# A hybrid decoder trunk on one core: block compression contracted over 128 rows, with shifted copies of keys and values

## The reference, cut to what matters

```python
CMP_LEN, CMP_STRIDE, dh, G = 32, 16, 64, 2
def _compress(x, idx, pe, w1, w2):          # x: (B, T, G, dh)
    blocks = x[:, idx] + pe[:, None, :]      # 31 windows of 32 positions, 16 apart
    blocks = jnp.swapaxes(blocks, 2, 3).reshape(B, idx.shape[0], G, -1)
    return jax.nn.silu(blocks @ w1) @ w2     # w1: (32*64, 64), w2: (64, 64)
kc = _rms_norm(_compress(k_cmp, cmp_idx, cmp_pe[0], cmp_w1[0], cmp_w2[0]), k_g[0])
vc = _compress(v_cmp, cmp_idx, cmp_pe[1], cmp_w1[1], cmp_w2[1])
```

## Time and profile before

| | |
|---|---|
| runs | 2716.51, 2718.03, 2720.47 us; median 2718.03 |
| span of the profiled execution | 2716.9 us (its own time is not among the three; the median lies 1.1 us above the span) |
| TensorE busy, matmul records | 2664.1 us, 98% of the span |
| granted clock of TensorE, mean | 0.995 |
| VectorE, GpSimd, ScalarE busy | 1326.2, 1230.2, 1100.5 us |
| the compression's matmuls (line 763) | 256 records in each of the 2 layers |

### The profile page before, as it was taken

How to read it: one execution, slowest core, us unless ns; L and a number is a source line. 1 busy time by engine, 2 the same in 40 slices (tenths; PEclk the granted TensorE clock), 3 DMA queues, 4 the chain that set the end, 5 groups by cost and what they waited for, 6 DMA issues and landing times.

```text
span 2716.9 us, 36975 instructions
## 1 busy us (share of the span) xinstructions
PE 2664.1 (98%) x13132; PEld 2137.3 (79%) x13132; DVE 1326.2 (49%) x1834; ACT 1100.5 (41%) x1664; POOL 1230.2 (45%) x616
## 2 busy tenths in 40 slices
PE   8999999989999999999999999999899999999999
PEld 6888888766678868888888888887667788788887
DVE  5221258786535554252541212777865364543533
ACT  5322242446644454222342223434476445542222
POOL 4444456672235424444444434567522354344443
PEclk9999999999999999999999999999999999999999
DMA  4334433222224313333333353432122342233332
GB/s 133 95 99 113 115 98 87 70 55 55 55 78 117 109 47 107 94 99 95 91 95 101 93 132 92 111 79 68 49 55 63 86 124 85 62 101 101 93 100 78
DMA packets 493612, 243.41 MB, mean 90 GB/s; under 512 B 49468, under 2 KB 491174, under 8 KB 493478
## 3 DMA queue, kind: packets, MB, share of 16 engines
q1 hardware_dynamic: 492960, 241.49, 32.0%
q10 hardware_dynamic: 518, 0.13, 0.0%
HBM read 239.46 MB, written 2.10 MB: 89 GB/s over the span
## 4 chain that ended last, share of the span: by engine, by line
PE 65%; issue 16%; POOL 8%; DVE 5%; ACT 3%; POOLq 2%; DVEq 1%; ACTq 0%; DMA 0%; SPq 0%
PE pg L636 20%; PE pg L639 19%; PE pg L642 19%; POOL wL L585 7%; PE pA L706 2%; DVE convb L1740 1%; PE pA L911 1%; PE pA L858 1%; POOLq L612 1%; POOLq L614 1%; DVE prob L1902 0%; POOL wsn L610 0%; ACT prob L1156 0%; ACT wH L1156 0%; ACT hH L1156 0%
## 5 line engine op out<-in xcount | busy, mean ns | idle before, releaser
L585 POOL TENSOR_TENSOR wL<-raw,wH 128x1024 fp32r<-128x1024 f32 (+1 forms) x472 | 1084.9, 2300 | 1453.2 <-ACT wH L1156 1449.4
L636 PE MATMUL pg<-gxH,wH 128*128 128x512 f32 (+1 forms) x2448 | 960.6, 392 | 3.6 <-DVE gxL L1601 3.1
L642 PE MATMUL pg<-gxH,wL 128*128 128x512 f32 (+1 forms) x2448 | 948.7, 388 | 0.0
L639 PE MATMUL pg<-gxL,wH 128*128 128x512 f32 (+1 forms) x2448 | 944.1, 386 | 0.0
L1156 ACT ACTIVATE wH<-raw 128x1024 fp32r<-128x1024 f32 (+1 forms) x472 | 475.8, 1009 | 834.3 <-PE pg L642 673.5
L636 PEld LDWEIGHTS pg<-gxH,wH 128*128 128x128 f32 x2448 | 461.0, 188 | 110.7 <-issue 18.4
L639 PEld LDWEIGHTS pg<-gxL,wH 128*128 128x128 f32 x2448 | 461.2, 188 | 93.6 <-issue 7.1
L642 PEld LDWEIGHTS pg<-gxH,wL 128*128 128x128 f32 x2448 | 461.0, 188 | 93.2 <-issue 3.9
L642 PE MATMUL pg<-hH,wL 128*128 128x512 f32 x992 | 392.7, 396 | 0.0
L636 PE MATMUL pg<-hH,wH 128*128 128x512 f32 x992 | 390.5, 394 | 1.5 <-DVE hL L1657 1.5
L639 PE MATMUL pg<-hL,wH 128*128 128x512 f32 x992 | 390.6, 394 | 0.0
(11 more groups left out here) (234 smaller groups left out, 2208.8 us busy)
## 6 DMA issues: line engine op xcount, KB each, us to landing
raw<-in_ffn_wi SPq DMA_DIRECT2D x352, 256.0 KB, 3.1
raw<-in_w_in SPq DMA_DIRECT2D x200, 256.0 KB, 3.3
raw<-in_ffn_wo SPq DMA_DIRECT2D x128, 256.0 KB, 3.0
raw<-in_ffn_wo SPq DMA_DIRECT2D x64, 192.0 KB, 2.6
raw<-in_xkv SPq DMA_DIRECT2D x32, 256.0 KB, 3.0
raw<-in_w_out SPq DMA_DIRECT2D x32, 256.0 KB, 3.0
raw<-in_sgu_out SPq DMA_DIRECT2D x32, 128.0 KB, 2.2
raw<-in_conv_out SPq DMA_DIRECT2D x32, 128.0 KB, 2.2
```

Of the source, the lines that this page charges most:

```text
L585: pool.tensor_tensor(wL[:, s % 4, 0:n, :], raw[:, s % 2, 0:n, :], wH[:, s % 4, 0:n, :].bitcast(F32), ALU.subtract)\
L636: mm(o, wH[:, s, k, :], rh(k), start=(k == 0), stop=False)
L639: mm(o, wH[:, s, k, :], rl(k), start=False, stop=False)
L642: last = mm(o, wL[:, s, k, :], rh(k), start=False, stop=(k == kt - 1))
```

## The change

The 32 positions of a window are contracted in pairs. Even positions' channels take rows 0 to 63, odd positions' channels rows 64 to 127, and both groups stand side by side as 62 columns. For that, each of the two halves needs each group's data: group 0 at even positions lies where it is needed, group 1 at odd positions too, and the other two are copied by four SBUF-to-SBUF transfers for each layer (`kvx`), the odd one shifted by a position. Keys' sums go to rows 0 to 63 of bank 2, values' to rows 64 to 127 of bank 3. `w1` is loaded once, with even positions on one half of the partitions and odd ones on the other; `w2` shrinks in the same way, and the small loads go from 18 to 12. The windows are built by eight additions of 64 x 496 instead of two of 128 x 992: four where the two stood, four after the keys' `normed(l, 2, ...)`, behind a wait for the copies. SyncE waits for `kv_in` between the loads of unit `U_KV + 4` and those of `U_KV + 5`, and issues the four copies there.

```diff
-        w1 = [[big[:, 0:2 * T], big[:, 2 * T:4 * T]], [prob[:, 0:2 * T], prob[:, 4 * T:6 * T]]]
-        w1 = [[half.rearrange("p (j e) -> p j e", j=HL) for half in both] for both in w1]
+        w1 = [t.rearrange("p (j e) -> p j e", j=HL) for t in (big[:, 0:2 * T], prob[:, 0:2 * T])]
+        kvx = [big[:, (2 + i) * T:(3 + i) * T] for i in range(2)]
         blk = [big[:, (4 + 2 * i) * T:(4 + 2 * i) * T + CMP_LEN * NCMP]
-               .rearrange("p (j n) -> p j n", j=CMP_LEN) for i in range(2)]
+               .rearrange("p (j g n) -> p j g n", j=HL, g=KVG) for i in range(2)]
...
-                        rows = cmp_w1[l][i].rearrange("(j d) e -> d j e", d=DH)
-                        for x in range(2):
-                            load_small(w1[i][x][r, :, :], rows[:, x * HL:(x + 1) * HL, :])
-                        load_small(w2[r, i, :], cmp_w2[l][i])
+                        rows = cmp_w1[l][i].rearrange("(j b d) e -> b d j e", b=2, d=DH)
+                        load_small(w1[i][r, :, :], rows[half])
+                    load_small(w2[r, 0, :], cmp_w2[l][half])
...
                 for i in range(6):
                     unit(l, U_KV + i, 0, cols_of(win, C_KV + i * P))
+                    if i == 4:
+                        sp.wait_ge(kv_in, risen(kv_in, l, 1))
+                        for j in range(2):
+                            sp.dma_start(kvx[j][0:DH, :], kvc[DH:P, j, :]).then_inc(kvx_in, 16)
+                            sp.dma_start(kvx[j][DH:P, 0:T - 1], kvc[0:DH, j, 1:T])\
+                                .then_inc(kvx_in, 16)
...
-                for i in range(2):
-                    for j in range(CMP_LEN):
-                        for g in range(KVG):
-                            r = slice(g * DH, (g + 1) * DH)
-                            last = mm(pA[r, 2 + g, 32 * i:32 * i + NCMP],
-                                      w1[i][j // HL][r, j % HL, :], blk[i][r, j, :],
-                                      start=(j == 0), stop=(j == CMP_LEN - 1))
+                for j in range(HL):
+                    for i in range(2):
+                        last = mm(pA[i * DH:(i + 1) * DH, 2 + i, 0:KVG * NCMP], w1[i][:, j, :],
+                                  blk[i][:, j, :, :].rearrange("p g n -> p (g n)"),
+                                  start=(j == 0), stop=(j == HL - 1))
                 last.then_inc(cmp1, 1)
...
-                    mm(pA[r, 3, 0:NCMP], w2[r, 0, :], hc[r, 0, 0:NCMP], start=True, stop=True)
+                    mm(pA[r, 3, 0:NCMP], w2[0:DH, 0, :], hc[0:DH, g, 0:NCMP], start=True, stop=True)
                 for g in range(KVG):
-                    r = slice(g * DH, (g + 1) * DH)
-
-                    last = mm(pA[0:NCMP, 3 - g, P:P + DH], hc[r, 1, 0:NCMP],
-                              w2[r, 1, :], start=True, stop=True)
+                    last = mm(pA[0:NCMP, 2, P + g * DH:P + (g + 1) * DH], hc[DH:P, g, 0:NCMP],
+                              w2[DH:P, 0, :], start=True, stop=True)
...
                 scaled(kvc[:, 1, :], l, U_KV + 1)
                 dve.drain()
 
+                dve.drain().then_inc(kv_in, 1)
+
+                def windows(i, g, half, src):
+
+                    src = bass.AP(tensor=src.tensor, offset=src.offset,
+                                  ap=[src.ap[0], [2, HL], [CMP_STRIDE, NCMP]])
+                    r = slice(half * DH, (half + 1) * DH)
+                    pe_ = par[r, P_PE + i * HL:P_PE + (i + 1) * HL]
+                    pe_ = bass.AP(tensor=pe_.tensor, offset=pe_.offset,
+                                  ap=[pe_.ap[0], [1, HL], [0, NCMP]])
+                    return TTt(blk[i][r, :, g, :], src, pe_, ALU.add)
+
                 for i in range(2):
-                    src = kvc[:, i, :]
-                    src = bass.AP(tensor=src.tensor, offset=src.offset,
-                                  ap=[src.ap[0], [1, CMP_LEN], [CMP_STRIDE, NCMP]])
-                    pe_ = par[:, P_PE + i * CMP_LEN:P_PE + (i + 1) * CMP_LEN]
-                    pe_ = bass.AP(tensor=pe_.tensor, offset=pe_.offset,
-                                  ap=[pe_.ap[0], [1, CMP_LEN], [0, NCMP]])
-                    last = TTt(blk[i], src, pe_, ALU.add)
-                last.then_inc(blk_in, 1)
+                    windows(i, 0, 0, kvc[0:DH, i, :])
+                    windows(i, 1, 1, kvc[DH:P, i, 1:T])
                 conv(2)
...
                 normed(l, 2, kT[:, 0, :], col(P_NK + 1))
+                dve.wait_ge(kvx_in, risen(kvx_in, l, 16 * 4))
+                for i in range(2):
+                    windows(i, 1, 0, kvx[i][0:DH, :])
+                    last = windows(i, 0, 1, kvx[i][DH:P, :])
+                last.then_inc(blk_in, 1)
                 scaled(kT[:, 1, :], l, U_KV + 4)
                 squares(kT[:, 1, :])
                 v_copied(0)
```

More of the change, by code:

```diff
@@ L116, in trunk @@
         eps = sb("eps", [P, 1])
-        w2 = sb("w2", [P, 2, DH])
+        w2 = sb("w2", [P, 1, DH])
         hc = sb("hc", [P, 2, 32])
@@ L129, in trunk @@
         mst = sb("mst", [P, 2])
-        NP_ROWS = 126
+        NP_ROWS = 94
         NPAR = NP_ROWS + 4 * CONV_W
@@ L281, in trunk @@
         hid_l = sig("hid_l", 2 * FT)
-        small = sig("small", 16 * 18)
+        small = sig("small", 16 * 12)
         memld = sig("memld", 16 * 1)
+        kv_in = sig("kv_in", 1)
+        kvx_in = sig("kvx_in", 16 * 4)
         blk_in = sig("blk_in", 1)
@@ L733, in v_rows @@
                     last.then_inc(v_tr, 1)
-                pe.wait_ge(small, risen(small, l, 16 * 18))
+                pe.wait_ge(small, risen(small, l, 16 * 12))
                 turn(pA[:, 0, 0:4 * CONV_W], cwt[0:4 * CONV_W, :], 4 * CONV_W).then_inc(cw_tr, 1)
@@ L1259, in _ @@
                               (nsa_k_norm.rearrange("l a c -> a l c"), P_NK),
-                              (cmp_pe.rearrange("l i a c -> i a l c")[0], P_PE),
-                              (cmp_pe.rearrange("l i a c -> i a l c")[1], P_PE + CMP_LEN)):
+                              (cmp_pe.rearrange("l i (a b) c -> i b a l c", b=2)[0, half], P_PE),
+                              (cmp_pe.rearrange("l i (a b) c -> i b a l c", b=2)[1, half], P_PE + HL)):
                     n = g.shape[0]
@@ L1297, in _ @@
                     last = act.activation(hc[r, :, 0:NCMP],
-                                          pA[r, 2 + g, 0:64].rearrange("p (i n) -> p i n", i=2)
-                                          [:, :, 0:NCMP], ACT.Silu)
+                                          pA[r, 2 + g, 0:KVG * NCMP]
+                                          .rearrange("p (g n) -> p g n", g=KVG), ACT.Silu)
                 last.then_inc(cmp_act, 1)
@@ L1810, in _ @@
                 dve.tensor_copy(kcn[:, 0:NCMP], pA[:, 3, 0:NCMP])
-                for g in range(KVG):
-                    dve.tensor_copy(vcs[0:NCMP, g, 0:DH], pA[0:NCMP, 3 - g, P:P + DH])
+                dve.tensor_copy(vcs[0:NCMP, :, 0:DH],
+                                pA[0:NCMP, 2, P:2 * P].rearrange("p (g d) -> p g d", g=KVG))
                 squares(kcn[:, 0:NCMP], NCMP)
```

## The result

The changed kernel takes 2724.8 us (median of 12 runs, 2722.56 to 2729.53); the kernel before takes 2718.03 beside it. The ratio is 1.0021, with a 95% interval from 1.0014 to 1.0028. It is slower by a little over what a measurement of this kernel can tell from no change, where 2711.8 and a gain were forecast. The profiled execution took 2722.56 us, 1.8 more than its span. It is the fastest of the twelve, 2.2 us under their median, so its rows show a little less than what the change costs in a typical execution.

The account below looks back on a forecast made before the run. TensorE, its matmul records covering 98% of the span, was taken to bound the kernel. A layer: -5.6 + 0.1 + 2.4 = -3.1 us; both layers -6.2, so 2718.0 becomes 2711.8 us, range 2706.5 to 2717.5.

Parts of the forecast that it names:

- back-to-back ones of VectorE keep their turn: VectorE and GpSimd: two-SBUF-input instructions exclude each other, and consecutive VectorE ones are not interrupted; read from a 3.93 us wait.
- the layout by hand: VectorE before the third statistic: late additions 456.1 to 459.9, squares end 462.9, statistic at 463.0 instead of 460.15.
- Rival 4: Late additions: GpSimd gets turns between them, pauses about 5.5 us, statistic 8 us late, 2723.0 us; chance 0.07.
- The loss at the statistic: TensorE waiting for VectorE's late squares at the third statistic: 2.4 us a layer taken, 0.7 to 4 in the forecast.
- rival 3: Third statistic: both waits on GpSimd are full, a loss of about 5 us a layer, 2717.0 us; chance 0.10.
- The compression: TensorE's compression matmuls: 32 pairs at 59 ns, 2.0 us instead of 7.58, saving 5.6 us a layer.
- rivals 2 and 5: Compression: 2, pairs take 4.1 us instead of 2.0, 2716.0 us, 0.10; 5, loads don't overlap, saving 0.5, 2722.0, 0.03.
- `w2`: Four small TensorE matmuls with w2: values' two now share rows and columns, +0.1 us a layer.
- The copies: Four SBUF-to-SBUF copies for each layer: landed by 445 us or so, waiting for them costs nothing.
- Unit `U_KV + 5`: Its load, held behind the copies: ready about 449 to 451 us, TensorE takes it at 454.6, so hidden.
- Smaller loads: Small loads, 12 instead of 18: SyncE's issue 6.1 us shorter, 1 MB a layer saved, no gain taken.

Follow-up runs that it names:

- The cut additions of the kernel before: Kernel before the change, its two additions of 128x992 cut into four of 128x496 in the same place; 2718.94 us, one run.
- filled stop: Changed kernel plus six 128x512 matmuls on constants on TensorE ahead of the third statistic; 2723.12 us, ratio 1.0014.
- merged: Changed kernel with keys' and values' additions merged, two early and two late of 64 x 992 at the same places; 2720.45 us, ratio 1.0006.
- without taps: Changed kernel with GpSimd's convolution taps starting seven units later, leaving only subtractions beside the late additions; 2728.56 us, ratio 1.0034.
- halves: Changed kernel with each group of four additions reordered, those on the same partition half together; 2724.16 us, ratio 1.0019.

## Why the prediction was wrong

**The step that failed is the rule "back-to-back ones of VectorE keep their turn".** It was read from one pair, where a tap waited 3.93 us, and the layout by hand ran the late four from 456.1 to 459.9 on it. They started at 456.25, close to the forecast, and ran until 464.45, since GpSimd had a turn at each. The cut additions of the kernel before show that the rule fails even where it was read, from the third addition on.

Rival 4 had this mechanism, and its total of 2723.0 us came near the measured 2724.8. That is in part luck. It put all of its 8 us into the wait for the squares; the wait was 5.8, the pauses in the additions some 4.1 instead of 5.5, and the 2.0 or 1.6 us of clock that filled up the sum were not in it. It was given 0.07, since none of the rows showed more than two in a row against a GpSimd with work queued. But the trace from which the rows were taken had such a case, in the attention of the first layer: four subtractions of 128 x 512 back to back, each with two SBUF inputs (VectorE first, then GpSimd).

```profile
564.54 0.69 DVE L1946 TENSOR_TENSOR hL<-big,hH 128x512 fp32r<-128x512 f32 x1
565.14 1.80 DVE L1946 TENSOR_TENSOR hL<-big,hH 128x512 fp32r<-128x512 f32 x1
566.86 0.68 DVE L1946 TENSOR_TENSOR hL<-big,hH 128x512 fp32r<-128x512 f32 x1
567.47 1.09 DVE L1946 TENSOR_TENSOR hL<-big,hH 128x512 fp32r<-128x512 f32 x1
...
564.59 1.81 POOL L613 TENSOR_TENSOR convb<-convb,wsn 128x512 f32<-128x512 f32 x1
566.56 1.46 POOL L610 TENSOR_SCALAR wsn<-convb,par 128x512 f32<-128x512 f32 x1 [0.17 <-issue]
```

A tap's sum gets in ahead of the second, which takes 1.80 us; a tap's product waits through the third and gets in ahead of the fourth, which takes 1.09. So before any run the rule already stood against a counterexample in its own trace, and rival 4's chance should have been far higher.

The Trainium skill, in "SBUF — State Buffer" (section "SBUF: two separate sides"), says only that a lock is held for one whole instruction. Nothing in it says that the next in the same queue keeps it; that was added by the prediction, from the 3.93 us, which span one addition and the next. The trace agrees with the page, in the 1.26 to 3.02 us of the late four, and not with the addition.

**A term was missing.** The loss at the statistic was sized 2.4 us, with 0.7 to 4 in the forecast and about 5 in rival 3. A stop also costs clock: 2.0 us in the first layer and 1.6 in the second. The forecast had TensorE at the same speed behind a stop as in front of it. With the longer stop, 7.4 to 7.8 us came where 2.4 stood.

**The sum, term by term for a layer.** The compression -5.6 as forecast (2.01 us measured for 32 pairs, 63 ns a pair over all). The reading of the earlier trace rows held, that such records do not pay for their load and their stream one after the other, which by the prediction's working would have been 7.1 us: rivals 2 and 5 fell. `w2` +0.1 as forecast. Statistic +7.8 and +7.4 instead of +2.4. Together +2.3 and +1.9 instead of -3.1.

**What was costed at nothing cost nothing.** The copies landed in 2.3 us. Unit `U_KV + 5`, held back by them, was split and ready at about 450.2, and TensorE took it at 455.69 without a wait, inside the forecast 449 to 451. Smaller loads gained nothing that can be told. With the late four left out, and with them moved away from the squares, 12.6 and 12.8 us a run came out for two layers of 5.5 by the working, which leaves 1.6 to 1.8 us to scatter.

**What stays open.** Why GpSimd sometimes waits through one more instruction of VectorE. In the traces of all these runs only a tap's product (line 610, 617 after the change) ever did, and only beside instructions on 128 partitions. Between the additions on 64 partitions the same product got in at the next gap (460.48 in the change). No run tells why.

## What to carry to other kernels

When an instruction is inserted ahead of something the bottleneck engine waits for with a small slack, count the instructions as well as their durations: each one of VectorE with two SBUF inputs may cost one instruction of a busy GpSimd. Put such work behind the waited-for step, or ahead of an idle stretch: the same additions at another place turned +0.2% into -0.5%. A rule read from a single pair of instructions is one sample; its rival deserves a chance that says so. Before a rule of that kind is used, the rest of the trace is worth a search for a case that breaks it. And a stop of the engine that bounds the kernel costs more than its length if its clock falls with it.

## What the runs showed of the hardware that was not expected

- Beside a GpSimd with work queued, VectorE's additions with two SBUF inputs mostly lost a turn each: 1.26 to 3.02 us instead of 1.01 for an addition of 64 x 496, 8.20 and 9.23 instead of 4.1 for four, 6.13 for two of twice the size. The exception is named above: one more instruction passed a waiting tap's product, on 128 partitions.
- After a stop of 5.8 us TensorE ran at 0.50 of its clock for some 3 us. What the clock cost, from the statistic to the compression, did not grow with the stop: 1.7 us behind a stop of 2.52 (filled stop, second layer), 3.0 behind 3.75 (merged), 2.5 behind 4.46 (without taps), 2.0 and 1.6 behind 5.8 (the change), 2.7 behind 7.67 (halves).
- Two streams of matmuls on different columns of the array with the same 128 rows took 2.01 us for 32 pairs of 62 columns, 63 ns a pair, near the 59 ns of the 31-column pairs on separate rows before: twice the columns and twice the rows in nearly the same time.
